# Three small experts of a mixture layer with high and low parts in one stationary operand, and a quarter of their low weights made on GpSimd

## The chip, the cores and the metric

The kernel runs on one core of a Trainium2 chip. A core has TensorE (PE) for matrix products, VectorE (DVE), ScalarE (ACT) and GpSimd (POOL) for elementwise work, and SyncE (SP), which here only issues DMAs. The metric is the device time in microseconds of one execution, as the median of several runs.

## The reference

A trunk of two layers over 256 tokens of width 1024. Each layer has a norm, an input projection, four mixers, an output projection, and then a feed-forward part: dense in layer 0, and a mixture of 8 experts in layer 1 of which each token uses two. The change is in the mixture alone:

```python
def swiglu(h, w1, w3, w2):
    return (jax.nn.silu(h @ w1) * (h @ w3)) @ w2

def moe_ffn(h, router_w, router_b, w1, w3, w2):
    logits = h @ router_w + router_b
    top_v, top_i = lax.top_k(logits, 2)
    top_w = jax.nn.softmax(top_v, axis=-1)
    combine = jnp.sum(jax.nn.one_hot(top_i, 8) * top_w[..., None], axis=-2)
    y = jnp.zeros_like(h)
    for e in range(8):
        y = y + combine[..., e:e + 1] * swiglu(h, w1[e], w3[e], w2[e])
    return y
```

Everything is float32. w1[e] and w3[e] are 1024x3584, w2[e] is 3584x1024.

## The kernel before

**Numbers of full precision.** TensorE multiplies fast in the type float32r, which keeps a part of the mantissa. So each operand is split: high is the value rounded to float32r, low is what is left. A product is then three matmuls, high·high, high·low and low·high (`three` in `one_expert`, lines L1323 to L1325).

**Tiling.** Each expert holds up to 128 tokens (`SLOTS`) as stationary operands x_high and x_low (128x128 blocks), and the weights are the moving operand, 512 columns at a time. An expert's weights are 21 chunks of 128x4096 numbers (2 MB); each chunk is two units of 128x2048, so an expert has 42 units (m = 0 to 41). Experts are taken in pairs: g is the pair (0 to 3), u the expert in it (0 or 1), and r = 2g + u. The order of a pair's units is fixed (`MOE_ORDER`): blocks of w1 and w3, with those of w2 between. `up` handles w1 and w3, `down` handles w2, `turn` transposes the gated activations so that `down` can use them as stationary operands.

**Who does what for a unit.**
- SP loads chunks into `ring`, which has 6 places; a place is free when PE has used it (`unit_used`).
- ACT makes w_high of unit m (`high`, L2547). There are 3 places for it (`HIGHS`), so ACT waits until PE has used unit m - 3.
- DVE makes the low part, ring_low = ring - w_high, 2048 columns (`low`, L2044), as soon as `high_made` says so.
- PE runs 12 matmuls of 512 columns, after `low_made`.

**Beside the units**, at numbers m written by hand in the loops of DVE and ACT (`two_experts`): ACT applies Silu to w1's sums (m = 6, 7, 15, 16, 26, 27, 36) and copies the turned activations to act_high (m = 14, 22, 34, 39); DVE multiplies with w3's sums (m = 9, 10, 18, 19, 30, 31, 37, L2105) and subtracts for act_low (m = 14, 22, 34, 39, L2110). At m = 2 and 4 DVE writes the result of the expert before, 128x1024, into act_m (L2056); GpSimd sends these rows to DRAM by an indirect DMA (`rows_out`, L842), and DVE waits at m = 9 until they have landed (`s_rows_out`), since its product at m = 9 writes act_m again. GpSimd also gathers the tokens of the next pair (`tokens_in`, L854), and in the last expert it reads the rows back, which DVE adds to x at m = 17, 20, 25, 28 (L2073). Other work GpSimd has none in this stage. The experts run in the order of their numbers.

## Time and profile before

| | |
|---|---|
| median of 3 runs | 1537.56 us (1536.78 to 1537.92) |
| profiled execution, span | 1535.7 us |
| granted TensorE clock, mean | 0.996 |
| PE busy | 1515.2 us |
| DVE busy | 1298.2 us |
| ACT busy | 968.0 us |
| POOL busy | 90.3 us |

The span is from the first to the last instruction; the timed runs lie about 1.9 us above it. The mixture's matmuls run from 559 us to the end. Ends of matmuls are modelled, so PE's busy time says little of itself; the distance from one matmul to the next shows the pace.

### The profile page before, as it was taken

How to read it: one execution, taken by the hardware profiler on the slowest of the kernel's cores; microseconds unless marked ns; L12 is line 12 of the kernel's file. 1: busy time of each engine (PE TensorE's matmuls, PEld its weight loads, DVE VectorE, ACT ScalarE, POOL GpSimd, SP SyncE). 2: the span in 40 equal slices, each digit the busy share in tenths (PEclk: the TensorE clock that was granted, in tenths of full speed). 3: DMA queues.
4: the chain of work that ended last, by engine and by line, in shares of the span. 5: the costliest groups of instructions: out<-in, count | busy, mean ns of one | idle time of the engine just before them, and what ended most of it. 6: DMA issues, size and time to landing. Idle time of an engine off the chain costs nothing.

```text
span 1535.7 us, 19169 instructions
## 1 busy us (share of the span) xinstructions
PE 1515.2 (99%) x7785; PEld 1236.0 (80%) x7785; DVE 1298.2 (85%) x1175; ACT 968.0 (63%) x841; POOL 90.3 (6%) x141
## 2 busy tenths in 40 slices
PE   8999999999999999999999999999999999999997
PEld 4886799999788568888888888888888888888885
DVE  5888887778885579988899999898998888998996
ACT  3532444444554357777777777787777787777775
POOL 5300100000000030100000100000010000000000
PEclk9999999999999999999999999999999999999999
DMA  9776698877823199999999999999999999999990
GB/s 347 285 254 239 231 359 323 304 288 274 310 94 131 55 312 391 377 385 386 354 363 385 369 392 391 354 364 382 367 390 376 376 357 375 382 364 372 411 368 30
DMA packets 161862, 494.13 MB, mean 322 GB/s; under 512 B 4587, under 2 KB 8855, under 8 KB 161767
## 3 DMA queue, kind: packets, MB, share of 16 engines
q1 hardware_dynamic: 156160, 474.76, 82.7%
q0 software_dynamic: 4928, 16.69, 3.1%
q8 instruction: 63, 1.03, 0.3%
q10 hardware_dynamic: 678, 1.40, 0.2%
q14 instruction: 33, 0.26, 0.1%
HBM read 483.91 MB, written 8.91 MB: 321 GB/s over the span
## 4 chain that ended last, share of the span: by engine, by line
PE 90%; DVE 6%; SPq 2%; DMA 1%; ACT 1%; issue 0%; DVEq 0%; ACTq 0%
PE bank L1323 20%; PE bank L1324 20%; PE bank L1325 20%; PE bank L975 4%; PE bank L1183 4%; PE bank L1224 3%; PE bank L1223 3%; PE bank L1222 3%; PE bank L972 2%; PE bank L1356 2%; PE bank L1198 1%; PE bank L1199 1%; PE bank L1200 1%; DMA ring<-in_w_mod_dram 1%; DVE ring_low L2044 1%; PE bank L998 1%
## 5 line engine op out<-in xcount | busy, mean ns | idle before, releaser
L2044 DVE TENSOR_TENSOR ring_low<-ring,w_high 128x2048 fp32r<-128x2048 f32 x336 | 768.6, 2293 | 95.1 <-ACT w_high L2547 89.0
L2547 ACT ACTIVATE w_high<-ring 128x2048 fp32r<-128x2048 f32 x336 | 646.6, 1926 | 228.8 <-PE bank L1325 220.3
L1323 PE MATMUL bank<-w_high,x_high 128*128 128x512 f32 x896 | 352.9, 394 | 0.1
L1324 PE MATMUL bank<-ring_low,x_high 128*128 128x512 f32 x896 | 351.4, 392 | 0.0
L1325 PE MATMUL bank<-w_high,x_low 128*128 128x512 f32 x896 | 348.9, 389 | 0.0
L1323 PEld LDWEIGHTS bank<-w_high,x_high 128*128 128x128 f32 x896 | 168.5, 188 | 37.4 <-DVE ring_low L2044 1.2
L1325 PEld LDWEIGHTS bank<-w_high,x_low 128*128 128x128 f32 x896 | 168.2, 188 | 37.4
L1324 PEld LDWEIGHTS bank<-ring_low,x_high 128*128 128x128 f32 x896 | 168.3, 188 | 34.7
L1323 PE MATMUL bank<-w_high,act_high 128*128 128x512 f32 x448 | 178.8, 399 | 0.2 <-DVE ring_low L2044 0.2
L2468 ACT ACTIVATE tmp_r<-ring 128x1024 fp32r<-128x1024 f32 x84 | 88.9, 1061 | 140.8 <-PE bank L1224 82.0
L1324 PE MATMUL bank<-ring_low,act_high 128*128 128x512 f32 x448 | 177.7, 397 | 0.0
L1325 PE MATMUL bank<-w_high,act_low 128*128 128x512 f32 x448 | 176.5, 394 | 0.0
L1889 DVE TENSOR_TENSOR ring_low<-ring,tmp_r 128x1024 fp32r<-128x1024 f32 x84 | 102.6, 1225 | 34.6 <-ACT tmp_r L2468 32.9
L1222 PE MATMUL bank<-h_high,tmp_r 128*128 128x256 f32 x448 | 125.7, 281 | 1.1 <-DVE h_low L1907 1.1
L1224 PE MATMUL bank<-h_low,tmp_r 128*128 128x256 f32 x448 | 125.9, 281 | 0.0
L1223 PE MATMUL bank<-h_high,ring_low 128*128 128x256 f32 x448 | 125.9, 281 | 0.0
L1323 PEld LDWEIGHTS bank<-w_high,act_high 128*128 128x128 f32 x448 | 84.2, 188 | 21.8 <-issue 0.9
L1325 PEld LDWEIGHTS bank<-w_high,act_low 128*128 128x128 f32 x448 | 84.2, 188 | 20.7
L1324 PEld LDWEIGHTS bank<-ring_low,act_high 128*128 128x128 f32 x448 | 84.2, 188 | 18.8
L1222 PEld LDWEIGHTS bank<-h_high,tmp_r 128*128 128x128 f32 x448 | 84.3, 188 | 2.4 <-issue 2.2
L1224 PEld LDWEIGHTS bank<-h_low,tmp_r 128*128 128x128 f32 x448 | 84.9, 189 | 0.0
L1223 PEld LDWEIGHTS bank<-h_high,ring_low 128*128 128x128 f32 x448 | 84.2, 188 | 0.4 <-issue 0.2
(381 smaller groups left out, 1657.3 us busy)
## 6 DMA issues: line engine op xcount, KB each, us to landing
ring<-in_moe_w_dram SPq DMA_DIRECT2D x168, 2048.0 KB, 9.1
ring<-in_w_mod_dram SPq DMA_DIRECT2D x23, 2048.0 KB, 12.9
ring<-in_ffn_w_dram SPq DMA_DIRECT2D x21, 2048.0 KB, 11.8
ring<-in_w_in_dram SPq DMA_DIRECT2D x7, 2048.0 KB, 13.6
ring<-in_w_out_dram SPq DMA_DIRECT2D x4, 2048.0 KB, 8.4
ring<-in_w_in_dram SPq DMA_DIRECT2D x4, 1024.0 KB, 15.5
ring<-in_w_mod_dram SPq DMA_DIRECT2D x2, 1024.0 KB, 15.7
gate_row<-in_b_mod_dram POOLq DMA_DIRECT2D x4, 512.0 KB, 7.6
```

What stands on the lines that cost most here:

```text
L975: ins = mm(b[:, i * T:(i + 1) * T], w[:, k, off + i * P:off + (i + 1) * P], h_t[:, k, :], start=k == 0, stop=k == KB - 1)
L1183: ins = mm(bank[2 * tt + half][:, :], y_t[:, i, tt * P:(tt + 1) * P], wide(("wout", l, half))[:, i, :], start=n == 0 and i == 2 * g, stop= ...
L1222: mm(o, w_h[:, k, :], h_high[:, k, :], start=k == 0, stop=False)
L1223: mm(o, w_l[:, k, :], h_high[:, k, :], start=False, stop=False)
L1224: ins = mm(o, w_h[:, k, :], h_low[:, k, :], start=False, stop=k == KB - 1)
L1323: mm(out_, x_h, w_h, start=first, stop=False)
L1324: mm(out_, x_h, w_l, start=False, stop=False)
L1325: return mm(out_, x_l, w_h, start=False, stop=last)
L1889: mark(tt_(quarter(ring_low, QUARTERS[m]), quarter(ring, QUARTERS[m]), quarter_high(m).bitcast(F32), ALU.subtract).then_inc(ffn_l.sem, 1), ...
L2044: tt_(moe_low(u, m // 2)[:, c], moe_slot(u, m // 2)[:, c], w_high[:, m % HIGHS, :].bitcast(F32), ALU.subtract).then_inc(low_made, 1)
L2468: mark(act(quarter_high(m), quarter(ring, QUARTERS[m]), ACT.Copy).then_inc(ffn_h.sem, 1), ffn_h, "q")
L2547: act(w_high[:, m % HIGHS, :], moe_slot(u, m // 2)[:, c], ACT.Copy).then_inc(high_made, 1)
```

## The change

- The first two experts are as before. The other six are put in an order by their number of tokens: the three with the fewest come second in the pairs 1, 2 and 3 (r = 3, 5, 7). SP reads the expert's number from memory once per expert and loads its weights from there. DVE works out the order in the first expert (`later_order`, called at m = 6 to 11).
- Such a small expert has room for 64 tokens. The stationary operand's 128 columns hold the 64 high parts and the 64 low parts of the same tokens. So two matmuls (w_high and w_low) do what three did; the result has 64 rows of high and 64 rows of low sums, which are added up later: for the gate and the product by a matmul with `fold` (128x64, two identities above each other), for the output by a second indirect DMA that adds (`compute_op=ALU.add`).
- In a small expert DVE subtracts the first 1536 columns of each unit, and GpSimd the last 512 (`low_rest`). PE waits for GpSimd's part before the last block of each unit (`rest`).
- Gate and product change: ACT copies both sums to SBUF, PE turns and adds them, ACT applies Silu to what PE made, DVE multiplies, ACT copies the high part, DVE subtracts.
- `rows_out` of a small expert is two indirect DMAs, the second issued when the first has landed; `s_rows_out` is now waited for at 16 * rows_before(r), which counts both.

```diff
+        def is_small(q, g, u):
+            return q == 0 and g > 0 and u == PAIR - 1
+        def rows_before(r):
+            return r + sum(is_small(0, n // PAIR, n % PAIR) for n in range(r))
...
+                    if later and i == 0:
+                        number_of = eng.value_load(order_i[0:1, e - FIRST:e - FIRST + 1], min_val=0, max_val=NE - 1)
...
+                if is_small(0, g, u):
+                    eng.indirect_dma_start(expert_rows[:, :], ... index[:, g % 2, 0, u, PAIR:PAIR + 1] ...)
+                    eng.wait_ge(s_rows_out, 16 * (rows_before(r) + 1))
+                    eng.indirect_dma_start(expert_rows[:, :], ... compute_op=ALU.add).then_inc(s_rows_out, 16)
...
+            def low_rest(g, u):
+                r = expert(0, g, u)
+                for m in range(UNITS):
+                    if m == ROWS_AT:
+                        rows_out(r - 1)
+                    if r == NE - 1 and m in ROWS_IN_AT:
+                        rows_in(ROWS_IN_AT.index(m))
+                    c0 = m % 2 * (KB * W // 2)
+                    c = slice(c0 + KB * W // 2 - W, c0 + KB * W // 2)
+                    eng.wait_ge(high_made, unit_at(r, m))
+                    eng.tensor_tensor(moe_low(u, m // 2)[:, c], moe_slot(u, m // 2)[:, c],
+                                      w_high[:, m % HIGHS, KB * W // 2 - W:].bitcast(F32),
+                                      ALU.subtract).then_inc(rest_made, 1)
...
+                def rest(m, last_block):
+                    if small_one and last_block:
+                        eng.wait_ge(rest_made, small_rep(g) * UNITS + m + 1)
                 def three(out_, x_h, x_l, w_h, w_l, first, last):
+                    if small_one:
+                        mm(out_, x_h, w_h, start=first, stop=False)
+                        return mm(out_, x_h, w_l, start=False, stop=last)
                     mm(out_, x_h, w_h, start=first, stop=False)
                     mm(out_, x_h, w_l, start=False, stop=False)
                     return mm(out_, x_l, w_h, start=False, stop=last)
...
                 def turn(j):
+                    if small_one:
+                        eng.wait_ge(even_a.sem, even_a.at(f"q{j}", small_rep(g)))
+                        for n, part in enumerate((act_s, act_m)):
+                            for hb in range(HB):
+                                c = n * HB * SMALL + hb * SMALL
+                                ins = mm(bank[6 + j % 2][:, c:c + SMALL], part[:, j % 2, hb * P:(hb + 1) * P], fold,
+                                         start=True, stop=True)
...
-            def low(r, u, m):
-                c = slice(m % 2 * (KB * W // 2), (m % 2 + 1) * (KB * W // 2))
+            def low(r, u, m, shared_one=False):
+                n = KB * W // 2 - (W if shared_one else 0)
+                c = slice(m % 2 * (KB * W // 2), m % 2 * (KB * W // 2) + n)
...
+                    def small_products(*js):
+                        for j in js:
+                            eng.wait_ge(moe_a.sem, moe_a.at(f"s{j}", r))
+                            done(eng, tt_(act_m[:, j % 2, 0:HB * SMALL], act_s[:, j % 2, 0:HB * SMALL],
+                                          bank[6 + j % 2][:, HB * SMALL:], ALU.mult) ...
+                        for j in js:
+                            eng.wait_ge(moe_a.sem, moe_a.at(f"ah{j}", r))
+                            done(eng, tt_(halves_of(j)[:, :, SMALL:], folded(act_m, j),
+                                          halves_of(j)[:, :, 0:SMALL].bitcast(F32), ALU.subtract) ...
...
                         if m == 9 and not first and not q:
-                            eng.wait_ge(s_rows_out, 16 * r)
+                            eng.wait_ge(s_rows_out, 16 * rows_before(r))
...
+                        if first and 6 <= m < 13:
+                            later_order(m - 6)
...
+                    def small_highs(*js):
+                        for j in js:
+                            eng.wait_ge(moe_t.sem, moe_t.at(f"t{j}", r))
+                            done(eng, act(act_s[:, j % 2, 0:HB * SMALL], bank[6 + j % 2][:, 0:HB * SMALL], ACT.Silu) ...
+                        for j in js:
+                            eng.wait_ge(moe_v.sem, moe_v.at(f"m{j}", r))
+                            done(eng, act(halves_of(j)[:, :, 0:SMALL], folded(act_m, j), ACT.Copy) ...
```

GpSimd's queue from the first gather of the mixture to the end. Before (L854 gathers tokens, L842 sends rows, L869 reads them back):

```order
L854 DMA xn<-token_rows,index 128x1024 x2
L842 DMA expert_rows<-act_m,index 640x1024 x2
L854 DMA xn<-token_rows,index 128x1024 x2
L842 DMA expert_rows<-act_m,index 640x1024 x2
L854 DMA xn<-token_rows,index 128x1024 x2
L842 DMA expert_rows<-act_m,index 640x1024 x3
L869 DMA x_slots<-expert_rows 128x2x1024 x2
```

Now, for the pairs 1 and 2 (L926 gathers, L914 sends rows, L904 and L909 are the two DMAs of a small expert, L951 is `low_rest`):

```order
L951 TENSOR_TENSOR ring_low<-ring,w_high 128x512 x6
L914 DMA expert_rows<-act_m,index 640x1024
L951 TENSOR_TENSOR ring_low<-ring,w_high 128x512 x36
L904 DMA expert_rows<-act_m,index 640x1024
L909 DMA expert_rows<-act_m,index 640x1024
L926 DMA xn<-token_rows,index 128x1024 x2
L951 TENSOR_TENSOR ring_low<-ring,w_high 128x512 x6
L914 DMA expert_rows<-act_m,index 640x1024
L951 TENSOR_TENSOR ring_low<-ring,w_high 128x512 x36
```

GpSimd, which had only DMAs to issue, has 42 subtractions per small expert, with the DMA of the expert before after six of them.

DVE's queue in the first half of a pair's second expert (u = 1). Before (L2044 is `low`, L2056 the result of the expert before, L2105 the product, L2110 act_low):

```order
L2056 TENSOR_TENSOR act_m<-bank,gate_row 128x512
L2044 TENSOR_TENSOR ring_low<-ring,w_high 128x2048 x5
L2105 TENSOR_TENSOR act_m<-act_s,bank 128x512
L2044 TENSOR_TENSOR ring_low<-ring,w_high 128x2048
L2105 TENSOR_TENSOR act_m<-act_s,bank 128x512
L2044 TENSOR_TENSOR ring_low<-ring,w_high 128x2048 x4
L2110 TENSOR_TENSOR act_low<-bank,act_high 128x512 x2
L2044 TENSOR_TENSOR ring_low<-ring,w_high 128x2048 x4
```

Now (L2215 is `low`, L2227 the result of the expert before, L2280 the product, L2285 the low part of the activations):

```order
L2227 TENSOR_TENSOR act_m<-bank,gate_row 128x512
L2215 TENSOR_TENSOR ring_low<-ring,w_high 128x1536 x10
L2280 TENSOR_TENSOR act_m<-act_s,bank 128x256 x2
L2285 TENSOR_TENSOR act_high<-act_m,act_high 128x4x64 x2
L2215 TENSOR_TENSOR ring_low<-ring,w_high 128x1536 x8
L2280 TENSOR_TENSOR act_m<-act_s,bank 128x256 x2
L2285 TENSOR_TENSOR act_high<-act_m,act_high 128x4x64 x2
```

The two products have moved from m = 9 and 10 to m = 14, just ahead of the two subtractions, and both are half as wide.

## Rows read from the trace of the kernel before

**Rows 1.** Page, part 5: engine, tiles, shapes, count; busy us, mean ns; idle before, releaser.
```profile
L2044 DVE TENSOR_TENSOR ring_low<-ring,w_high 128x2048 fp32r<-128x2048 f32 x336 | 768.6, 2293 | 95.1 <-ACT w_high L2547 89.0
L2547 ACT ACTIVATE w_high<-ring 128x2048 fp32r<-128x2048 f32 x336 | 646.6, 1926 | 228.8 <-PE bank L1325 220.3
```

**Rows 2.** Windows: stretch, us; busy of PE, PEld, DVE, ACT, POOL; clock; DMA share; GB/s.
```profile
691.10:811.50 120.40, 120.40 (x546) 98.48 (x545) 106.44 (x62) 93.14 (x67) 2.36 (x1) 1.00 0.99 368
...
700.00:710.00 10.00, 10.00 (x45) 8.23 (x44) 9.41 (x7) 6.76 (x4) 0.00 (x0) 1.00 1.03 416
```

**Rows 3.** Timeline of PE: start us, duration us, instruction; two matmuls, 32 places apart.
```profile
559.75 0.39 PE L1323 MATMUL bank<-w_high,x_high 128*128 128x512 f32 x1
...
567.07 0.39 PE L1325 MATMUL bank<-w_high,x_low 128*128 128x512 f32 x1
```

**Rows 4.** Timeline of ACT, expert r = 2: the high of m = 12.
```profile
707.35 1.93 ACT L2547 ACTIVATE w_high<-ring 128x2048 fp32r<-128x2048 f32 x1 [0.87 <-PE bank L1325]
```

**Rows 5.** Timelines of POOL, then DVE, 541 to 549 us: both subtract.
```profile
541.97 2.36 POOL L824 TENSOR_TENSOR h_high<-xn,xn_high 128x1024 fp32r<-128x1024 f32 x1 [2.12 <-PE bank L941]
544.93 3.75 POOL L824 TENSOR_TENSOR h_high<-xn,xn_high 128x1024 fp32r<-128x1024 f32 x1 [0.59 <-ACT xn_high L2361]
...
543.88 2.60 DVE L2044 TENSOR_TENSOR ring_low<-ring,w_high 128x2048 fp32r<-128x2048 f32 x1
...
547.73 0.99 DVE L1987 TENSOR_TENSOR route<-route,route_c 128x16 f32<-128x16 f32 x1
...
549.79 0.17 DVE L1987 TENSOR_TENSOR route<-route,route_c 128x16 f32<-128x16 f32 x1
```

**Rows 6.** Timelines of POOL, then DVE, 39 to 56 us: small subtractions.
```profile
39.77 0.46 POOL L797 TENSOR_TENSOR band_a<-band_a,consts 128x128 f32<-128x128 f32 x1
...
53.90 0.81 POOL L797 TENSOR_TENSOR band_b<-band_b,consts 128x128 f32<-128x128 f32 x1
...
53.69 0.69 DVE L1714 TENSOR_TENSOR tmp<-tmp 128x512 f32<-128x512 f32 x1
54.42 0.56 DVE L1718 TENSOR_TENSOR tmp<-tmp 128x256 f32<-128x256 f32 x1
55.02 0.42 DVE L1719 TENSOR_TENSOR tmp<-tmp 128x256 f32<-128x256 f32 x1
```

**Rows 7.** Timeline of DVE: an instruction with one input in PSUM beside POOL's of 541.97.
```profile
541.56 2.28 DVE L1658 TENSOR_SCALAR h_t<-bank,mod_col 128x256 f32<-128x256 f32 x4 [1.13 <-PE bank L941]
```

**Rows 8.** Timelines of ACT, then of DVE, and a group: other pieces.
```profile
558.52 0.42 ACT L2536 ACTIVATE x_high<-x_slots 128x256 fp32r<-128x256 f32 x1 [1.18 <-DVE x_slots L2184]
...
692.69 0.58 ACT L2573 ACTIVATE act_s<-bank 128x512 f32<-128x512 f32 x1
...
L2073 DVE SCALAR_TENSOR_TENSOR x<-x_slots,route_c,x 128x1024 f32<-128x1024 f32 x4 | 5.1, 1280 | 0.0
```

**Rows 9.** Timeline of DVE, expert r = 2: the product at m = 9.
```profile
703.22 0.68 DVE L2105 TENSOR_TENSOR act_m<-act_s,bank 128x512 f32<-128x512 f32 x1
```

**Rows 10.** Timeline of POOL: the row DMAs; what ended the idle time before each.
```profile
691.11 2.36 POOL L842 DMA_INDIRECT expert_rows<-act_m,index  x1 [51.87 <-DVE act_m L2056]
...
1413.17 2.34 POOL L842 DMA_INDIRECT expert_rows<-act_m,index  x1 [116.84 <-DVE act_m L2056]
1422.74 0.77 POOL L869 DMA_DIRECT2D x_slots<-expert_rows  x1 [7.24 <-DMA expert_rows<-act_m,index]
```

**Rows 11.** DMA issues: count, KB each, median us to landing; the second of these adds.
```profile
token_rows<-xn_high POOLq DMA_DIRECT2D x1, 1024.0 KB, 6.7
token_rows<-h_high POOLq DMA_DIRECT2D x1, 1024.0 KB, 8.5
```

**Rows 12.** Windows as in rows 2: 6 us during and after short pauses of PE.
```profile
552.00:558.00 6.00, 5.54 (x29) 4.71 (x29) 3.43 (x8) 2.11 (x5) 1.27 (x1) 0.72 0.54 154
```

**Rows 13.** Timeline of DVE, expert r = 0: the lows of m = 7 to 9, and of 12.
```profile
576.28 6.92 DVE L2044 TENSOR_TENSOR ring_low<-ring,w_high 128x2048 fp32r<-128x2048 f32 x3 [1.57 <-ACT w_high L2547]
...
589.21 2.29 DVE L2044 TENSOR_TENSOR ring_low<-ring,w_high 128x2048 fp32r<-128x2048 f32 x1 [0.15 <-ACT w_high L2547]
```

More of the change, by code:

```diff
@@ L206 @@
         ("lgt lg max0 eq0 cand0 first0 pick0 lg2 max1 eq1 cand1 first1 pick1 sel diff ch1 ch0 one w1 w2 sw1 sw2 wt ch2 "
-         "most most_i idle row0 row1 token0 token1").split(),
+         "count idle row0 row1 token0 token1").split(),
+    "perm_v":
+        ("key less rank lot over pos some count most most_i hot at order_f order sel2 at0 put0 at1 put1 row0 row1").split(),
+    "even_a":
+        ("p0 p1 q0 q1 p2 p3 q2 q3 p4 p5 q4 q5 p6 q6").split(),
     "route_a":
@@ L1347, in up @@
                                 for jj in range(n_j):
+                                    rest(m, (kk, jj) == (per - 1, n_j - 1))
                                     c = slice(jj * W, (jj + 1) * W)
@@ L1370, in down @@
                             for bb in range(HB // 2):
+                                rest(m, (half, bb) == (1, HB // 2 - 1))
                                 hb = part * HB // 2 + bb
@@ L1388, in last_down @@
                             for bb in range(HB // 2):
+                                rest(m, (half, bb) == (1, HB // 2 - 1))
                                 hb = part * HB // 2 + bb
@@ L2587, in two_experts @@
                                  spread_a, "s", at)
+                        if m in (10, 18, 30, 38) and small_one:
+                            j = 2 * (10, 18, 30, 38).index(m)
+                            for n in range(j, min(j + 2, NJ)):
+                                copy_value(n)
                         if m == 14:
-                            act_highs(0)
-                            act_highs(1)
+                            if small_one:
+                                small_highs(0, 1)
+                            else:
+                                act_highs(0)
+                                act_highs(1)
                         if m in (15, 16):
```

273 lines of the change are left out of this document (217 added, 56 removed).

## The prediction

> **What bounds the kernel now.** I read the page's busiest groups first, then windows of one expert each, then the timelines of PE, ACT and DVE inside a unit. An expert takes 120.35 us; six equal steps of rows like [rows 2] give that, with the clock at 1.00. Two matmuls 32 places apart start 7.32 us apart [rows 3], 0.229 us each, so a unit of 12 takes 2.745 us, and 42 units 115.3 of the 120.35; the rest is turning. ACT's high takes 1.926 us and waits for PE before nearly every unit (220 us of idle); DVE's low takes 2.293 us and waits for ACT [rows 1]. So PE sets the pace in a normal expert. DVE follows closely: 2.29 of 2.745 us. DMA moved 368 GB/s in that expert, and 416 in one stretch of 10 us [rows 2], so it isn't at its end.
>
> **What the change takes away.** In three of eight experts a unit has 8 matmuls: 8 × 0.229 = 1.83 us, 77 us an expert, with the new turns below 90. If only PE counted, each would be 30 us shorter. What is next? ACT's 1.926 us a unit, and the pair of subtractions, which is the question here.
>
> **Do DVE and GpSimd subtract side by side?** GpSimd's subtraction of 1024 columns took 2.36 us beside a DVE instruction with PSUM input, but 3.75 us when it came while DVE ran a low: that low ended at 546.48, GpSimd at 548.68, 2.20 us later. The reverse stands there too. DVE's small subtraction at 547.73 took 0.99 us instead of 0.17 and ended at 548.72, with GpSimd; and the low at 543.88, begun before GpSimd's first one ended at 544.33, took 2.60 us, ending 2.15 us after that [rows 5]. Again at 54 us: GpSimd begins at 53.90 during a DVE subtraction that ends at 54.38, and takes 0.81 us instead of 0.46; DVE's next one of 256 columns takes 0.56 instead of 0.42 and ends 0.27 us after GpSimd [rows 6]. So two subtractions with both inputs in SBUF run one after the other, whole; only the start-up (about 0.15 us each) is hidden by waiting.
>
> The Trainium skill (SBUF — State Buffer, Who interferes with whom) says that the second to issue fully blocks, but also that a DVE instruction with at most one SBUF input doesn't contend. The trace agrees: the four PSUM reads at 541.56 took 2.28 us, 0.57 each, beside GpSimd [rows 7]. By the page the new products (one input in PSUM) cost nothing beside GpSimd; counted as blocked they would add 7 × 0.42 us an expert.
>
> **Price of a unit's pair.** DVE: 2048 columns minus the start-up take 2.14 us, 1.046 ns a column, so 1536 take 1.61. GpSimd: from 128 columns in 0.46 us [rows 6] to 1024 in 2.36 [rows 5] is 2.12 ns a column, so 512 take 1.09. One after the other 2.69 us; with both start-ups unhidden 3.03; fully side by side, the longer of ACT's 1.93 and DVE's 1.76. I take 2.69, since the three blocked cases show the start-up hidden. PE has 1.83 us of work in 2.69. ACT's high of m + 3 is done 1.83 + 1.93 = 3.8 us after low m, and wanted after 6.5. So the pair sets the pace: 42 × 2.69 = 113.1 us.
>
> **The places at m = 14, 22, 34, 39.** Before, DVE multiplied at m = 9 and 10, and ACT made the next high meanwhile. Now at m = 14 DVE ends its low, multiplies (0.42), ACT copies (0.42) [rows 8, 6], twice and interleaved, about 1.4 us until ACT begins the next high; 1.93 more, then DVE's 1.7: 5.0 us from low to low instead of 2.69. That is 2.3 us, three times, and 1.8 with the single step at m = 39: 8.7 us. It could be nothing if ACT had a high in store, but it stands behind those copies in ACT's queue. Copies of the sums (14 of 0.58 us [rows 8]) fit into ACT's 0.76 us a unit and its lead; the 8 more turns per step are in PE's slack. GpSimd's DMA issue of 2.34 us at m = 6 [rows 10] lets DVE go ahead and costs about 0.7 us.
>
> Small expert: 113.1 + 8.7 + 0.7 = 122.5. r = 3 and 5 also fill the next pair's x_low, 1.1 us between lows: 123.6 each, +3.3 over 120.35. r = 7 adds the rows to x with four instructions of 1.28 us [rows 8], both inputs in SBUF, that were in slack: + 4.5, so 127.0, +6.7. Together **+13.3 us**.
>
> **The second row DMA.** Before, the rows of r = 1 were issued at 691.11 [rows 10], and DVE's wait at m = 9 ended at once, as its product began at 703.22 right behind the low [rows 9]. A row DMA lands about 9.5 us from its issue (1413.17 to 1422.74, where GpSimd waits for it) [rows 10]. After r = 3 and r = 5 the second is issued only then, and needs 9.5 us, or 11.3 if adding costs the 1.8 us by which the adding DMA to token_rows was longer [rows 11]. So DVE is free at 691.1 + 19.3 to 21.1 = 710.4 to 712.2 on the clock of r = 2. Behind its wait stand the product (0.7) and the low of m = 10 (2.29): 713.4 to 715.2. PE had finished unit 9 at 707.3, when it let ACT begin the high of m = 12 [rows 4]. PE stands still for 6.1 to 7.9 us; I take 7.7, since the new DMA adds. After short pauses of PE the granted clock was 0.72 over 6 us [rows 12]: of its two levels, 1.2 and 2.4 GHz, the lower for 3.4 us, which takes 6 × 0.28 = 1.7 us. 9.4 us, in r = 4 and r = 6: **+18.8 us**. Its bounds: nothing, if the DMAs land twice as fast; 22 with both high ends.
>
> **The order of the experts.** 21 small instructions in r = 0: 17 of 0.21 us (0.17 [rows 5] and the way to the next) and 4 on 144 numbers of 0.35, 5.0 us. After low 6 DVE idles 1.57 us [rows 13], which hides the first six; behind low 9 and before low 12 there is next to none (0.15) [rows 13], and the lead over PE is about 1 us. **+2 us** (0 to 5). SP's reads of the expert's number come many units ahead of need. The zeroing of one more block of rows and GpSimd's six new constants lie before m = 14 and are waited for by nobody earlier.
>
> **The sum.** 1535.7 + 13.3 + 18.8 + 2 = 1569.8 for the profiled span; the runs lie 1.9 above: **1571.7 us**, +2.2%.
>
> **Rivals.**
> *B, the subtractions overlap.* Then ACT bounds a small expert: 42 × 1.93 + 14 × 0.58 + 14 × 0.42 + fills of 6 = 101, with waits at the four places 104 us; 3 × -16.3 = -49, with the row DMAs' +19 and +2: **1509 us**, faster. For it: only a few overlaps are in the trace, and on GpSimd spans are rough. Against it: they all say the same, in both directions. It decides at the pair's time: with the stalls as I have them, the whole change breaks even at about 2.42 us a unit instead of 2.69, thus if a quarter of GpSimd's 1.09 us ran beside DVE.
> The Trainium skill (SBUF — State Buffer, A bandwidth-pool intuition that's wrong) gives about 358 GB/s between HBM and a core. By that an expert's 44.0 MB would take 123 us and no small expert could be shorter than before; the trace's 416 GB/s [rows 2] contradicts it, so it takes nothing from B.
> *C, nothing is hidden.* The pair takes 3.03 us: 14.3 us more per small expert, 43 in all: **1615 us**; if besides the clock fell in PE's gaps within small experts (0.9 us a unit, about 3 at the four places), a unit at half clock would be 8 × 0.43 = 3.4 us, and it is worse still. Against it: the start-ups were hidden in all cases.
> *D, a wash.* The row DMAs land early enough that DVE hardly waits, and the pair is a little faster than 2.69, down to 2.55: within 0.2%, **1537 us**.
>
> **Chances.** My forecast 0.67, B 0.15, C 0.11, D 0.07. 0.2% (3 us) is about what a measurement of this kernel can tell from no change. Faster by over 0.2%: 0.15 (B). Within: 0.07 (D). Slower: 0.78 (my forecast and C). My forecast by itself spans 1548 (no stalls beyond 3 us each, pair as taken, half the places) to 1597 (half of the start-ups unhidden). The range takes in D and most of C and leaves B out: 1534 to 1614.
>
> **What the next profile would show.** Right: in r = 3, 5, 7 GpSimd's and DVE's subtractions end alternately, low to low about 2.7 us, GpSimd's mean well over 1.3 us since it waits for DVE, or DVE's over 1.76; small experts of 122 to 127 us; r = 4 and r = 6 some 9 us longer than 120.35, with a gap on PE behind unit 9 and DVE waiting for expert_rows; r = 0 2 us longer. Wrong: DVE's lows of 1536 columns at 1.76 us and GpSimd's at 1.3 us in the same stretch, small experts near 104 us (B), or r = 4 as long as r = 2 (the second DMA is hidden).

## The result: 3.9% slower, and the profile after

| | before | after |
|---|---|---|
| median | 1537.74 us (1536.78 to 1538.52, 4 runs) | 1594.69 us (1593.5 to 1599.88, 4 runs) |
| profiled execution, span | 1535.7 us | 1597.9 us |
| granted TensorE clock, mean | 0.996 | 0.967 |
| DVE busy | 1298.2 us | 1317.5 us |
| POOL busy | 90.3 us | 390.3 us |

The ratio is 1.0385, with a 95% interval of 1.0365 to 1.0406 (the two medians by themselves give 1.037). The profiled execution of the changed kernel is the one of 1599.88 us, the slowest of its four, 5.2 us above their median. The forecast was 1571.7 us with a range of 1534 to 1614: the direction and the range hold, and the size is 23 us short.

One name in the parts ahead is wrong and touches no number. The stretch from 691 to 811 us of before, called there the expert r = 2 or its rows those of r = 1, is the expert r = 1, which sends the rows of r = 0.

I measured each expert from the second write of a result by DVE (at m = 4 of the next expert, L2056 before and L2227 after) to the next such write. For r = 7 the interval ends in the same way at the last result. In us:

| r | 1 | 2 | 3 small | 4 | 5 small | 6 | 7 small |
|---|---|---|---|---|---|---|---|
| before | 121.2 | 119.6 | 121.2 | 119.7 | 121.2 | 119.2 | 111.1 |
| after | 121.0 | 118.9 | 134.0 | 128.5 | 133.8 | 129.4 | 126.5 |

The differences add up to the 62.2 us between the two profiled spans: 1.9 before the mixture's first matmuls, 2.2 in r = 0, 12.8 + 12.6 + 15.4 = 40.8 in the small experts, 8.8 + 10.2 = 19.0 in r = 4 and r = 6, and -1.7 in the rest.

The groups of the page of after that answer to [rows 1] (columns as there; "+1 forms" means that two shapes share the row). L2215 is DVE's `low`, L951 GpSimd's `low_rest`, L1424 PE's first matmul in a small expert:

```profile
L2215 DVE TENSOR_TENSOR ring_low<-ring,w_high 128x2048 fp32r<-128x2048 f32 (+1 forms) x336 | 785.2, 2353 | 113.8 <-ACT w_high L2751 108.4
L2751 ACT ACTIVATE w_high<-ring 128x2048 fp32r<-128x2048 f32 x336 | 641.7, 1920 | 237.0 <-PE bank L1428 164.4
L951 POOL TENSOR_TENSOR ring_low<-ring,w_high 128x512 fp32r<-128x512 f32 x126 | 293.9, 2350 | 266.6 <-ACT w_high L2751 265.4
...
L1424 PE MATMUL bank<-w_high,x_high 128*128 128x512 f32 x336 | 146.4, 436 | 55.0 <-DVE ring_low L2215 49.7
```

The same groups by shape, from 560 to 1600 us, after:

```profile
L2215 DVE TENSOR_TENSOR ring_low<-ring,w_high 128x2048 fp32r<-128x2048 f32 x207 | 473.5, 2292 | 56.1 <-ACT w_high L2751 52.1
L2215 DVE TENSOR_TENSOR ring_low<-ring,w_high 128x1536 fp32r<-128x1536 f32 x126 | 304.8, 2454 | 55.6 <-ACT w_high L2751 54.2 <-DMA expert_rows<-act_m,index 0.5
```

DVE has a quarter fewer columns in a small expert and yet takes longer for them: 2454 ns for 1536, against 2292 for 2048. That is time in which the instruction stands and waits for GpSimd, as in the few cases of [rows 5]. The timelines of DVE, then of POOL, in r = 3 show it (start us, duration us, instruction, count; in brackets the idle time ahead of it and what ended it):

```profile
950.59 10.83 DVE L2215 TENSOR_TENSOR ring_low<-ring,w_high 128x1536 fp32r<-128x1536 f32 x4 [0.25 <-ACT w_high L2751]
961.35 0.86 DVE L2280 TENSOR_TENSOR act_m<-act_s,bank 128x256 f32<-128x256 f32 x2
962.37 0.95 DVE L2285 TENSOR_TENSOR act_high<-act_m,act_high 128x256 fp32r<-128x256 f32 x2 [0.16 <-ACT act_high L2798]
964.77 8.37 DVE L2215 TENSOR_TENSOR ring_low<-ring,w_high 128x1536 fp32r<-128x1536 f32 x3 [1.45 <-ACT w_high L2751]
973.41 1.76 DVE L2215 TENSOR_TENSOR ring_low<-ring,w_high 128x1536 fp32r<-128x1536 f32 x1 [0.28 <-ACT w_high L2751]
```

```profile
964.75 1.27 POOL L951 TENSOR_TENSOR ring_low<-ring,w_high 128x512 fp32r<-128x512 f32 x1 [2.17 <-ACT w_high L2751]
...
973.46 2.87 POOL L951 TENSOR_TENSOR ring_low<-ring,w_high 128x512 fp32r<-128x512 f32 x1 [1.93 <-ACT w_high L2751]
```

Not held up, DVE's instruction takes 1.76 us (973.41) and GpSimd's 1.27 (964.75). GpSimd's of 973.46 begins 0.05 us after DVE's, and ends 1.16 us after it, having taken 2.87. In the steady stretch at 950.59 four lows take 10.83 us: 2.70 us a unit, where 1.76 + 1.27 is 3.03, so 0.33 us of start-up is hidden.

### The profile page after: what moved, and what is told of

Its sections match the earlier page's. It is cut to its first block, busy times and chain, and to the rows that moved or that the text cites. A ratio compares the mean times of both kernels' runs of the same rounds, so it can differ in the third digit from the quotient of the medians.

```text
span 1597.9 us, 19147 instructions
## 1 busy us (share of the span) xinstructions
PE 1479.0 (93%) x7533; PEld 1189.2 (74%) x7533; DVE 1317.5 (82%) x1199; ACT 978.0 (61%) x883; POOL 390.3 (24%) x276
## 4 chain that ended last, share of the span: by engine, by line
PE 65%; DVE 14%; ACT 7%; DMA 5%; POOL 4%; issue 4%; SPq 1%; ACTq 0%; DVEq 0%; POOLq 0%
PE bank L1426 10%; PE bank L1427 10%; PE bank L1428 10%; DVE ring_low L2215 10%; PE bank L1068 5%; ACT w_high L2751 4%; DMA expert_rows<-act_m,index 4%; PE bank L1276 4%; POOL ring_low L951 3%; PE bank L1317 3%; PE bank L1316 3%; PE bank L1315 3%; PE bank L1065 3%; PE bank L1424 2%; PE bank L1425 1%
## 5 line engine op out<-in xcount | busy, mean ns | idle before, releaser
L2215 DVE TENSOR_TENSOR ring_low<-ring,w_high 128x2048 fp32r<-128x2048 f32 (+1 forms) x336 | 785.2, 2353 | 113.8 <-ACT w_high L2751 108.4
L951 POOL TENSOR_TENSOR ring_low<-ring,w_high 128x512 fp32r<-128x512 f32 x126 | 293.9, 2350 | 266.6 <-ACT w_high L2751 265.4
L1426 PE MATMUL bank<-w_high,x_high 128*128 128x512 f32 x560 | 223.1, 398 | 17.3 <-DVE ring_low L2215 17.0
L1427 PE MATMUL bank<-ring_low,x_high 128*128 128x512 f32 x560 | 221.4, 395 | 0.0
L1428 PE MATMUL bank<-w_high,x_low 128*128 128x512 f32 x560 | 219.7, 392 | 0.0
L1424 PE MATMUL bank<-w_high,x_high 128*128 128x512 f32 x336 | 146.4, 436 | 55.0 <-DVE ring_low L2215 49.7
L1425 PE MATMUL bank<-ring_low,x_high 128*128 128x512 f32 x336 | 139.7, 416 | 0.0
L1426 PEld LDWEIGHTS bank<-w_high,x_high 128*128 128x128 f32 x560 | 106.4, 190 | 43.0 <-DVE ring_low L2215 19.3
L1424 PEld LDWEIGHTS bank<-w_high,x_high 128*128 128x128 f32 x336 | 68.2, 203 | 87.4 <-DVE ring_low L2215 63.8
L1428 PEld LDWEIGHTS bank<-w_high,x_low 128*128 128x128 f32 x560 | 106.1, 190 | 23.9
L1427 PEld LDWEIGHTS bank<-ring_low,x_high 128*128 128x128 f32 x560 | 106.3, 190 | 21.8
L1428 PE MATMUL bank<-w_high,act_low 128*128 128x512 f32 x280 | 110.8, 396 | 0.0
L1426 PE MATMUL bank<-w_high,act_high 128*128 128x512 f32 x280 | 110.6, 395 | 0.0
L1427 PE MATMUL bank<-ring_low,act_high 128*128 128x512 f32 x280 | 109.5, 391 | 0.0
L1424 PE MATMUL bank<-w_high,act_high 128*128 128x512 f32 x168 | 77.1, 459 | 25.7 <-DVE ring_low L2215 25.6
```

The source lines that it names most:

```text
L951: eng.tensor_tensor(moe_low(u, m // 2)[:, c], moe_slot(u, m // 2)[:, c], w_high[:, m % HIGHS, KB * W // 2 - W:].bitcast(F32), ALU.subtract ...
L1424: mm(out_, x_h, w_h, start=first, stop=False)
L1425: return mm(out_, x_h, w_l, start=False, stop=last)
L1426: mm(out_, x_h, w_h, start=first, stop=False)
L1427: mm(out_, x_h, w_l, start=False, stop=False)
L1428: return mm(out_, x_l, w_h, start=False, stop=last)
```

## What takes the 13 us of a small expert: a sum along DVE

From the result of r = 2 to that of r = 3 (933.5 to 1067.6 us), DVE's timeline of after divides so:

| stretch | by the measured pair of 2.70 us | measured |
|---|---|---|
| 10 lows, m = 5 to 14 | 27.0 | 27.1 |
| 8 lows, m = 15 to 22 | 21.6 | 21.7 |
| 12 lows, m = 23 to 34, with two subtractions for x_low | 32.4 | 37.2 |
| 5 lows, m = 35 to 39, with the third | 13.5 | 15.8 |
| 3 lows, m = 40 and 41 and the next expert's m = 0 | 8.1 | 8.1 |
| places behind m = 14, 22, 34, 39 | | 3 x 3.42 + 2.99 = 13.3 |
| the next expert's first 4 lows and results | | 10.9 |

The total is 134.1. The pair's pace is as forecast. Two lines are not: the places cost 13.3 us where 8.7 stood in the sum, and the stretches m = 23 to 39 lose 7.1 us where 1.1 stood for the fills. (The forecast's 0.7 us for GpSimd's DMA issue belongs to the first stretch, and nearly none of it shows there.)

**A place.** The rows above show it: DVE's low of m = 14 ends at 961.3, then two products, two subtractions, and 1.45 us of waiting for ACT's next high; the next low begins at 964.77. That is 3.42 us in which no low runs. The low of m = 15 then takes 2.86 us, since GpSimd's of 964.75 began just ahead of it.

**The long stretch.** ACT makes the next pair's tokens there ("fills"). Its timeline of after, r = 3, and DVE's beside it:

```profile
1014.58 1.15 ACT L2728 ACTIVATE x_slots<-bank,mod_col 128x256 f32<-128x256 f32 x2
1015.76 1.91 ACT L2751 ACTIVATE w_high<-ring 128x2048 fp32r<-128x2048 f32 x1
1017.58 1.15 ACT L2728 ACTIVATE x_slots<-bank,mod_col 128x256 f32<-128x256 f32 x2
1018.76 1.91 ACT L2751 ACTIVATE w_high<-ring 128x2048 fp32r<-128x2048 f32 x1
```

```profile
1014.71 1.76 DVE L2215 TENSOR_TENSOR ring_low<-ring,w_high 128x1536 fp32r<-128x1536 f32 x1 [1.23 <-ACT w_high L2751]
1017.71 1.76 DVE L2215 TENSOR_TENSOR ring_low<-ring,w_high 128x1536 fp32r<-128x1536 f32 x1 [1.24 <-ACT w_high L2751]
1020.70 1.76 DVE L2215 TENSOR_TENSOR ring_low<-ring,w_high 128x1536 fp32r<-128x1536 f32 x1 [1.24 <-ACT w_high L2751]
1022.38 2.98 DVE L2180 TENSOR_TENSOR x_low<-x_slots,x_high 128x256 fp32r<-128x256 f32 x2
```

ACT is at work without a pause: a high and two fills are 3.0 us, and so the lows come every 3.0 us. DVE waits 1.24 us for each high; its low then takes 1.76 us, unblocked. Then the two subtractions for x_low, both inputs in SBUF, take 2.98 us instead of the 0.88 that they take where GpSimd subtracts nothing (the first experiment below): GpSimd's subtraction stands in their way too.

A part of the loss is neither. Ahead of these rows, at m = 26 to 28, the lows come 3.6 to 3.7 us apart, and there ACT's highs waited for PE, which was behind after a stretch at the lower clock (0.50 from 992 to 998 us):

```profile
996.66 1.91 ACT L2751 ACTIVATE w_high<-ring 128x2048 fp32r<-128x2048 f32 x1 [3.30 <-PE bank L1425]
...
1000.35 1.93 ACT L2751 ACTIVATE w_high<-ring 128x2048 fp32r<-128x2048 f32 x1 [1.29 <-PE bank L1425]
```

What the clock takes in these stretches is measured by the matmuls at the places, below.

## Experiments: which part costs what

Two things had to be told apart: whether the shared run of the two subtractions sets the pace or the wait of PE for GpSimd, and what fills the rest of the 13 us. Each quoted expectation gives its own theories.

**GpSimd subtracts nothing.** VectorE takes all 2048 columns; the rest of the change stays.

```diff
+SHARE = 0
...
-                    eng.tensor_tensor(moe_low(u, m // 2)[:, c], moe_slot(u, m // 2)[:, c], ...
...
-                    if small_one and last_block:
-                        eng.wait_ge(rest_made, small_rep(g) * UNITS + m + 1)
...
-                n = KB * W // 2 - (W if shared_one else 0)
+                n = KB * W // 2 - (SHARE if shared_one else 0)
```

> In the three small experts VectorE subtracts all 2048 columns of a unit and GpSimd none; PE waits for VectorE alone. Nothing else is changed. Theory 1 (the two subtractions take turns at one SBUF port, 1.61 + 1.09 = 2.7 us a unit): VectorE alone needs 2.25 us a unit, so 42 x 0.45 = 19 us less in each small expert, 3 us more where GpSimd no longer holds up the fills; about 1530 us, faster than the changed kernel by 60. Theory 2 (the subtractions run side by side, and the copies at m = 14, 22, 34, 39 with their clock falls are what costs): VectorE has a third more to do in each unit and GpSimd's part was free, so it is slower than the changed kernel or the same, 1595 us or more.

It took 1544.83 us (1543.76 to 1546.0), ratio to before 1.0051 (1.0034 to 1.0068): 50 us less than the change, and 15 above the 1530 that its first theory gave. The small experts took 117.3, 117.8 and 106.8 us. So the subtraction on GpSimd is what makes them slow, although GpSimd takes work off DVE. They are also only 3 to 4 us shorter than before the change, although PE has a third less to do. DVE's lows in r = 3:

```profile
L2209 DVE TENSOR_TENSOR ring_low<-ring,w_high 128x2048 fp32r<-128x2048 f32 x43 | 96.7, 2288 | 13.5 <-ACT w_high L2745 13.0
```

DVE's own 96.7 us are now the larger part of the expert, and of the 13.5 us of idle time nearly all is for ACT's highs.

**GpSimd subtracts 256 columns instead of 512.**

```diff
+SHARE = 256
...
-                    c = slice(c0 + KB * W // 2 - W, c0 + KB * W // 2)
+                    c = slice(c0 + KB * W // 2 - SHARE, c0 + KB * W // 2)
...
-                n = KB * W // 2 - (W if shared_one else 0)
+                n = KB * W // 2 - (SHARE if shared_one else 0)
```

> GpSimd subtracts 256 columns of each unit in the small experts instead of 512, VectorE 1792 instead of 1536. Theory 1: the pair takes 1.87 + 0.54 = 2.41 us instead of 2.70, so 12 us less in each small expert, about 1560 us, between the changed kernel and the one where VectorE subtracts all. Theory 2: no gain, 1595 us or a little more.

1569.38 us (1564.45 to 1572.9), ratio 1.0207 (1.0179 to 1.0236), small experts 122.9, 124.0 and 114.3 us: 10 to 12 us less each, near the 12 expected, and the run 9 us above the 1560. Half the share costs about half of the 50 us. POOL's group, from 560 to 1600 us, shows that most of the instruction is waiting: half the columns take 1887 ns instead of 2350.

```profile
L952 POOL TENSOR_TENSOR ring_low<-ring,w_high 128x256 fp32r<-128x256 f32 x126 | 236.3, 1887 | 292.5 <-ACT w_high L2752 291.8
```

**GpSimd subtracts beside, and nobody waits for it.** VectorE takes all 2048 columns. GpSimd subtracts 512 columns of two other tiles once a unit; its result isn't used. Its first one in each small expert waits until PE has ended the expert before.

```diff
-                    eng.tensor_tensor(moe_low(u, m // 2)[:, c], moe_slot(u, m // 2)[:, c], ...
+                    eng.tensor_tensor(y_low[:, 0:W], gate_row[:, 0:W], final_row[:, 0:W],
                                       ALU.subtract).then_inc(rest_made, 1)
```

> The changed kernel with VectorE subtracting all 2048 columns of a unit, while GpSimd, once a unit in r = 3, 5, 7, subtracts 512 columns of two other tiles in SBUF (gate_row and final_row) into a tile that is not in use; nobody on PE's side waits for it and its result isn't used. It measures what GpSimd's subtraction costs VectorE when neither data nor a wait of PE ties the two. Theory 1 (the two engines' instructions with both inputs in SBUF run one after the other): a unit takes 2.14 + 1.09 = 3.23 us, small experts about 136 to 142, VectorE's lows show up to 3.4 us, and the run takes 1544.8 + 55 to 65 = 1600 to 1610. Theory 2 (they read side by side, and the change loses by PE's wait for a slow GpSimd): lows stay at 2.29 and the run at 1545, as with GpSimd subtracting nothing.

**The same with a memset**, which reads nothing.

```diff
-                    eng.tensor_tensor(y_low[:, 0:W], gate_row[:, 0:W], final_row[:, 0:W], ALU.subtract)
+                    eng.memset(y_low[:, 0:W].bitcast(F32), 0.0)
```

> As the run beside it, but GpSimd's instruction is a memset of 512 columns: it reads nothing from SBUF, only writes. The result isn't used. Theory 1 in its narrow form (only instructions with two SBUF inputs block each other): 1545, as with GpSimd doing nothing in these units. If any GpSimd instruction blocks VectorE, or its waits and semaphores cost by themselves, the small experts lengthen as in the run beside it, by its own duration of some 0.5 us a unit: 1565 and above.

Beside the subtraction the run takes 1652.51 us (1645.63 to 1653.86), ratio 1.0735 (1.0701 to 1.077), with small experts r = 3 and 5 of 149.8 and 147.7 us. Beside the memset it takes 1546.39 us (1544.69 to 1548.06), ratio 1.006 (1.0041 to 1.008), as with GpSimd doing nothing. From 960 to 1560 us, first POOL and DVE beside the subtraction, then beside the memset:

```profile
L954 POOL TENSOR_TENSOR act_low<-gate_row,final_row 128x512 fp32r<-128x512 f32 x96 | 253.9, 2645 | 210.4 <-ACT w_high L2754 202.2
...
L2216 DVE TENSOR_TENSOR ring_low<-ring,w_high 128x2048 fp32r<-128x2048 f32 x179 | 488.7, 2762 | 37.4 <-ACT w_high L2754 35.4
```

```profile
L954 POOL MEMSET act_low<- 128x512 f32 x110 | 57.9, 527 | 373.1 <-ACT w_high L2753 372.6
...
L2215 DVE TENSOR_TENSOR ring_low<-ring,w_high 128x2048 fp32r<-128x2048 f32 x194 | 438.7, 2289 | 58.7 <-ACT w_high L2753 56.3
```

With no common data and no wait of PE, GpSimd's subtraction of two SBUF tiles still lengthens DVE's lows; writing alone leaves them at 2289 ns. In a steady stretch eight lows beside the subtraction took 26.5 us, 3.31 a unit, near the sum of the two (2.14 + 1.09 = 3.23). The kernel lost more than the 55 to 65 us expected, 108 over the run in which GpSimd did nothing, and again not by the pair's pace: 38 lows at 3.31 are 125.8 us, and with the 13.3 us of the places and the next expert's start of 10.9 they give the 150 us that r = 3 took. The expectation had left the last two nearly out.

**Copies one unit later.** ACT copies the high activations, and DVE subtracts for the low ones, behind the next high and low (m = 15, 23, 35, 40), so that the next high doesn't stand behind them.

```diff
+                        if small_one and m in (15, 23, 35, 40):
+                            j = 2 * (15, 23, 35, 40).index(m)
+                            small_copies(*range(j, min(j + 2, NJ)))
```

> In the small experts ScalarE copies the high part of the gated activations, and VectorE subtracts for the low part, one unit later: behind the high and the low of m = 15, 23, 35 and 40. Silu and product stay where they are. Theory A (ScalarE's next high stood behind a copy that waits for VectorE's product, so VectorE and PE ran dry and the clock fell): the gaps of about 2.3 us at four places and the half clock behind them go, 12 to 16 us less in each small expert, 1548 to 1558 us; the granted clock stays near 1.0 in them. Theory B (the pace of the subtractions is all there is): under 5 us in all, 1590 to 1595 us.

1579.07 us (1576.13 to 1580.96), ratio 1.0274 (1.0253 to 1.0294): 16 us less than the change, between the two expectations. Small experts 126.2, 127.2 and 121.6 us. A place with it, DVE, r = 3:

```profile
959.05 0.86 DVE L2280 TENSOR_TENSOR act_m<-act_s,bank 128x256 f32<-128x256 f32 x2
960.53 2.88 DVE L2215 TENSOR_TENSOR ring_low<-ring,w_high 128x1536 fp32r<-128x1536 f32 x1 [0.62 <-ACT w_high L2756]
963.34 0.87 DVE L2287 TENSOR_TENSOR act_high<-act_m,act_high 128x256 fp32r<-128x256 f32 x2
```

Two products and the wait are 1.48 us instead of 3.42, and the subtractions come back as 0.9 to 2 us behind the low. The lows of the long stretch still come every 3.0 us. The small experts lose 7.8, 6.6 and 4.9 us of the 12.8, 12.6 and 15.4 by which they had grown: 61, 52 and 32%. Not all of that is the place's order by itself: without the stops at the places the granted clock in r = 3 is 0.99 instead of 0.91, and what that is worth comes below.

**A tile of its own for the rows.** The small expert's result goes to DRAM from another tile (it lies in the place of act_low, which is free until m = 14 of the next expert), and DVE's wait for the row DMAs moves to m = 14.

```diff
                 rows = act_m[:, :, :].rearrange("p a n -> p (a n)")
                 if is_small(0, g, u):
+                    rows = row_tile[:, :, :].rearrange("p a n -> p (a n)")
...
-                        if m == 9 and not first and not q:
+                        if m == (14 if is_small(0, (r - 1) // PAIR, (r - 1) % PAIR) else 9) and not first and not q:
```

> The rows of the experts r = 3 and 5 go out from the place of act_low, which is free until m = 14 of the next expert, and VectorE waits for the two row DMAs at m = 14 instead of m = 9 there. Theory: the wait is over by then, PE's gap behind unit 9 of r = 4 and r = 6 and the half clock behind it go, 9 to 10 us each, about 1576 us. If the two DMAs cost in another way (through the DMA engines, or GpSimd's queue), there is no gain, 1595 us.

1575.79 us (1573.28 to 1579.84), ratio 1.0249 (1.0232 to 1.0267), 19 us less, as expected. r = 4 and r = 6 are 118.9 and 118.5 us instead of 128.5 and 129.4; the small experts stay at 134.0, 133.7 and 126.5. DVE at m = 9 and 10 of r = 4, of after and then of this run:

```profile
1079.05 2.32 DVE L2215 TENSOR_TENSOR ring_low<-ring,w_high 128x2048 fp32r<-128x2048 f32 x1 [0.37 <-ACT w_high L2751]
1089.00 0.69 DVE L2294 TENSOR_TENSOR act_m<-act_s,bank 128x512 f32<-128x512 f32 x1 [7.63 <-DMA expert_rows<-act_m,index]
```

```profile
1079.35 2.29 DVE L2219 TENSOR_TENSOR ring_low<-ring,w_high 128x2048 fp32r<-128x2048 f32 x1 [0.37 <-ACT w_high L2756]
1081.56 0.68 DVE L2299 TENSOR_TENSOR act_m<-act_s,bank 128x512 f32<-128x512 f32 x1
```

**The clock, by two more matmuls a unit.** Behind each place PE's matmuls start 0.43 us apart, the pace at 1.2 GHz, for some units: in r = 3 that is about 24 us in all (a mean of 0.91 over 134 us, between the levels 0.50 and 1.00). Three matmuls of after behind the first place, and a window behind the second (columns as in [rows 2]):

```profile
967.68 0.79 PE L1424 MATMUL bank<-w_high,x_high 128*128 128x512 f32 x1 [3.38 <-DVE ring_low L2215]
968.27 0.63 PE L1425 MATMUL bank<-ring_low,x_high 128*128 128x512 f32 x1
968.70 0.63 PE L1424 MATMUL bank<-w_high,x_high 128*128 128x512 f32 x1
```

```profile
992.00:994.00 2.00, 1.22 (x3) 1.04 (x4) 2.00 (x2) 1.36 (x1) 2.00 (x2) 0.50 1.03 396
```

PE had stood still for 3.4 us ahead of the first. Does the lower clock cost anything? Zeros as a stationary operand keep PE busier without changing a sum. GpSimd writes the zeros at the start of each small expert, when PE has ended the expert before; n counts the blocks of matmuls, four in a unit.

```diff
+                    if m == 0:
+                        eng.wait_ge(unit_used, used_at(r, -1))
+                        eng.memset(act_low[:, 0, 0:P].bitcast(F32), 0.0).then_inc(s_clear, 1)
...
                     if small_one:
                         mm(out_, x_h, w_h, start=first, stop=False)
...
+                        if n % 4 in (1, 2):
+                            mm(out_, act_low[:, 0, 0:P], w_h, start=False, stop=False)
```

> The changed kernel with two more matmuls in each unit of r = 3, 5, 7: a stationary operand of zeros, made by GpSimd once an expert in act_low (which a small expert doesn't use), against w_high, added into the same sums, so nothing that is computed changes. PE's work in a unit goes from 1.83 to 2.29 us at the full clock, still below the 2.70 us of the pair of subtractions. Theory C (the clock at 1.2 GHz behind PE's stops costs time by itself: in r = 3 it lasts about 24 us in all, in which a unit takes 3.44 us instead of 2.70, so 7 units lose 0.74 each): with its stops shorter PE keeps the clock of 2.4 GHz and each small expert is about 5 us shorter, 129 instead of 134, the run about 1579 to 1584. Theory L (the clock only falls where PE would wait anyway, and what costs is that ACT and VectorE have no lead): no gain, or 0 to 5 us more per small expert since PE catches up less: 1595 to 1610.

> The same two matmuls with zeros per unit, on the kernel whose copies and subtractions of the activations come one unit later (1579.1 without them; r = 3, 5, 7 of 126.2, 127.2, 121.6 us, and the lower clock over about 4 us only in r = 3). There is next to no half clock left to win, so by both theories 1577 to 1584; if filling PE's gaps brings as much here as on the changed kernel itself, then it isn't by the clock.

On the changed kernel 1602.8 us (1601.24 to 1603.95), ratio 1.0441 (1.0423 to 1.0458), with small experts of 132.7, 133.9 and 127.2; on the one with later copies 1595.42 us (1592.72 to 1596.2), ratio 1.0392 (1.0375 to 1.0409), with 130.6, 128.9 and 126.8 instead of 126.2, 127.2 and 121.6. The first is where theory L had it. The second missed its expectation by 11 us and spoils the first as a proof: the edit costs something itself where there is next to no low clock to win back. So the extra matmuls were put only where PE stands still.

**The clock, by matmuls at the places only.** 12 matmuls with zeros before units 15, 23 and 35, 8 before unit 40; GpSimd writes the zeros as before.

```diff
+                            if small_one and m in (15, 23, 35):
+                                keep_busy(bank[first][:, :], 12)
                             eng.wait_ge(low_made, unit_at(r, m))
...
+                    if small_one and 2 * i == 40:
+                        keep_busy(bank[4][:, :], 8)
```

> The changed kernel; in r = 3, 5, 7 PE gets matmuls with zeros only where it stands still at the four places (12 of 0.229 us before unit 15, 23 and 35, 8 before unit 40, moving operand x_high, added into the sums, so nothing that is computed changes). Two matmuls in every unit kept the clock but cost PE's catching up elsewhere; these lie in stops of about 3.4 us. If the clock behind the places costs what the stretches behind m = 22 and m = 34 showed with the clock kept (1.7 and 0.8 us shorter), each small expert is 2 to 3 us shorter and the run 1586 to 1589 where the changed kernel again takes 1594.7. If half clock is hidden (the pair of subtractions is the pace at either clock), it takes the same within 2 us.

> The changed kernel as it is, on the same chip beside the run with matmuls at the places: 1594.7 as before (1593.5 to 1599.9), small experts of 134.0, 133.8, 126.5 us.

1595.89 us (1589.26 to 1600.35) with them, 1594.24 (1591.62 to 1596.53) without, ratios to before 1.0385 (1.0355 to 1.0415) and 1.0371 (1.0351 to 1.0391). One window over r = 3 of each, with them and then without (columns as in [rows 2]):

```profile
934.40:1064.80 130.40, 111.45 (x520) 85.84 (x521) 116.83 (x63) 97.05 (x81) 85.04 (x39) 1.00 0.92 341
```

```profile
932.10:1066.20 134.10, 109.16 (x476) 84.85 (x477) 109.64 (x63) 96.90 (x81) 91.07 (x39) 0.91 0.89 334
```

The clock stays at 1.00 instead of 0.91, and this expert is 3.7 us shorter. All of it lies in the two stretches m = 23 to 34 and 35 to 39: 34.6 and 14.5 us instead of 37.1 and 15.8. In r = 5 (0.97 instead of 0.91) the same two stretches are 3.3 us shorter together, and the expert takes 132.4 instead of 134.2. In r = 7, where ACT makes no fills, they take 49.7 and 49.4 us, so nothing is won, though the clock is 0.95 instead of 0.90, and the expert takes 127.7 instead of 125.3.

The edit has a price of its own that hides the gain in the sum. The interval of r = 2 ends four units into r = 3, where GpSimd waits and writes the zeros: it is 120.1 us instead of 118.9, and 120.2 in both runs with two more matmuls a unit. In r = 5 and r = 7 the stretch m = 5 to 14 is 1.1 us longer than without, and DVE waits there for the row DMA, which it doesn't without (1.80 and 1.65 us). Over the whole run nothing is won that can be measured: the expected 1586 to 1589 was missed, and the two runs are within 2 us, as if the half clock were hidden, though in two experts it isn't. So in r = 3 and r = 5 the lower clock takes part in the loss, with 3.3 to 3.7 of the 13 us, each from one profiled execution; it isn't the main cause. Of the 7.1 us lost in r = 3 at m = 23 to 39, 3.2 are left with the clock kept.

**Three edits together.** GpSimd subtracts nothing, copies one unit later, a tile of its own for the rows: the diffs above.

> Three edits of the changed kernel at once: VectorE subtracts all 2048 columns of a unit and GpSimd none; ACT's copies of the high activations and VectorE's subtraction for the low ones come one unit later (m = 15, 23, 35, 40); the row before goes through a tile of its own, and VectorE waits for the rows at m = 14 instead of m = 9. Everything is computed. By the single edits: GpSimd subtracting nothing gave 1544.8 with experts r = 3, 5, 7 at 117.3, 117.8, 106.8 us; a tile of its own took 9.5 and 10.9 us from r = 4 and r = 6; the later copies took 7.8, 6.6 and 4.9 us from the small experts, of which part hung on the shared port. If the effects add: 1544.8 - 20 = 1525 with the tile, and 3 to 15 us less with the copies, so 1510 to 1522, which is below the kernel of before (1537). If VectorE (2.14 to 2.29 us a unit, 90 to 96 us an expert, and its products) is the bound of a small expert by itself, the copies bring nothing and it is 1525. Rival: the gaps return elsewhere and it stays at 1537 or above.

1522.35 us (1520.42 to 1523.04), ratio 0.99 (0.9877 to 0.9924): faster than before by 1%, just above the 1510 to 1522 expected, and 72 us faster than the change. The experts are 121.0, 119.0, 115.5, 119.0, 115.8, 118.6 and 105.8 us. The gains add: the row tile's 20 us, and 2 us more by the copies, which bring little once the shared subtraction is gone. The window over r = 3:

```profile
933.50:1049.10 115.60, 101.74 (x477) 77.50 (x477) 102.22 (x62) 96.82 (x81) 2.36 (x1) 1.00 1.01 387
```

PE, DVE and ACT are each busy for 97 to 102 of 115.6 us, and the DMA engines' share is 1.01. No engine waited for a DMA in this window, and SP, which issues the loads, waited 105.6 us in it for PE to free places of the ring. DVE waited 12.8 us for ACT's highs, and ACT 13.8 for PE. No engine's work alone explains the rest of the time; which of them would have to be relieved next wasn't tried.

## Why the prediction was right in kind and too small

- **That PE sets the pace before, by little: borne out.** With GpSimd's part gone, a third less work for PE shortened a small expert by 3 to 4 us only, and DVE's lows and ACT's highs wait for each other. The new places are in that number too.
- **That two subtractions with both inputs in SBUF run one after the other: right**, in both directions, and it doesn't need common data or a wait. The rule of the Trainium skill (SBUF — State Buffer, Who interferes with whom), that the second to issue is fully blocked, holds here with 1.27 us becoming 2.87. So does its other half: DVE's two products at 961.35, with one input in PSUM, took 0.86 us while GpSimd's subtraction, held back by the low before them, ran on until 962.6.
- **2.69 us a unit: right.** 2.70 was measured in steady stretches, so 0.33 us of start-up is hidden, as taken. Rival B (side by side, 1509) and rival C's own mechanism (no start-up hidden, 3.03 us) are both out.
- **The four places, 8.7 us: too small.** They took 13.3 us. The step that failed is "1.93 more, then DVE's 1.7: 5.0 us from low to low instead of 2.69". The time without a low was nearly right, 1.4 + 1.93 = 3.3 us where 3.42 was measured. But the low behind the place was priced as if it had no partner. GpSimd waited for the same high and began first (964.75), and DVE's low took 2.86 us, not 1.7. So a place costs its whole 3.42 us on top of the pace, and not 2.3.
- **Fills, 1.1 us: too small.** 7.1 us were lost in the stretches with fills. Two things stand behind it. The step "1.1 us between lows" counted DVE's fills at their unblocked price and left out ACT's, which with the high take 3.0 us a unit there; DVE's three x_low subtractions took 4.75 us in r = 3. That is 3.2 us, the loss that was left with the clock kept. The rest, 3.7 to 3.9 us, went with the lower clock behind the places, which the sum put at nothing.
- **r = 7, +6.7 us: too small**, at +15.4. The places count here too, 4.6 us more than forecast. Its four additions to x, with both inputs in SBUF, had been priced at 1.28 us each, and two of them were held up by GpSimd's subtractions, 2.1 us in all (mean 1801 ns instead of 1280). The last 2 us weren't broken down.

```profile
L2246 DVE SCALAR_TENSOR_TENSOR x<-x_slots,route_c,x 128x1024 f32<-128x1024 f32 x4 | 7.2, 1801 | 0.0
```

- **The second row DMA, 9.4 us each in r = 4 and r = 6: right**, 8.8 and 10.2, and 9.6 and 10.9 by the run with the tile of its own. DVE was expected free at 19.3 to 21.1 us after the first DMA's issue. In r = 4 POOL issued it at 1069.14, and DVE went on at 1089.00, 19.9 us later, 9.9 for each of the two. In r = 6 it was 22.1 us, above that range: 10.0 for the first and 12.0 for the adding one, whose issue on GpSimd took 3.63 us instead of 1.56. In the repeated run both pairs took 19.9 and 19.8. So adding costs nothing in some cases and about 2 us in others; what decides it stays open.

```profile
1069.14 2.33 POOL L904 DMA_INDIRECT expert_rows<-act_m,index  x1 [15.84 <-DVE act_m L2227]
1079.05 1.56 POOL L909 DMA_INDIRECT expert_rows<-act_m,index  x1 [7.59 <-DMA expert_rows<-act_m,index]
```

PE stood still for 6.78 us before its next matmul (7.7 had been taken), and the rest of the 8.8 is what came behind: the granted clock was 0.50 from 1092 to 1096 us and 0.65 in the 2 us after (1.7 us had been taken for it, and 2.0 are left of the 8.8).

```profile
1092.07 0.80 PE L1426 MATMUL bank<-w_high,x_high 128*128 128x512 f32 x1 [6.78 <-DVE ring_low L2215]
```

- **The order of the experts, +2 us: right.** From the mixture's first matmul to the result of r = 0 it is 132.7 us instead of 130.6. The 1.9 us ahead of the mixture differ from run to run: 0.4 in the repeated run of the changed kernel, and with GpSimd subtracting nothing the mixture's first matmuls came 1.8 us earlier than before the change.
- **The lower clock inside small experts** stood only in a clause of rival C. It does occur, in r = 3 for some 24 us, and costs 3.7 us there and 3.3 in r = 5, in stretches where ACT has no lead; in r = 7 nothing was won by keeping it up. The mean clock of 0.967 shows PE's waiting more than it explains the loss.

The small experts took 40.8 us more instead of 13.3, which is 27.5 of the 28.1 us between the forecast span of 1569.8 and the profiled one of 1597.9. The profiled execution lay 5.2 us above the median, and so the medians' miss is 23. The direction was right for the reason given. That the time lay in the range is partly luck: its upper end came from rival C and the forecast's own span up to 1597 from half of the start-ups unhidden, and neither happened; the places, the fills and the clock filled that room.

## What to carry to other kernels

Here, work moved from VectorE to GpSimd saved nothing, since the instructions of both read two SBUF operands: the pair took the sum of the two, less the start-up, and VectorE's other such instructions in the same stretch got longer too. Before giving GpSimd a share, ask which of VectorE's instructions read an input from PSUM, as the products here, which were not held up, and let those lie beside it. And when an engine stops being the bound, go through every other engine's smaller pieces again at the new pace: what stood in the slack of 2.745 us a unit (ACT's fills, copies ahead of the next high, a second DMA behind the first) has to be priced in full.

## What the runs showed of the hardware that was not expected

- GpSimd's write of 512 columns (0.53 us) costs VectorE nothing beside it (lows of 2289 ns), while its subtraction of the same width does (2762 ns). The prediction hadn't asked; the narrow form of that experiment's theory had it so. A GpSimd instruction with a single SBUF input wasn't run.
- The indirect DMA that adds took 9.95 us from its issue to DVE going on in r = 4 and 12.0 in r = 6 of the same execution, where the plain ones ahead of them took 9.9 and 10.0.
- Extra matmuls in PE's waiting time weren't free: 0.46 us of them a unit, with the zeros that GpSimd writes for them, cost 16 us with the later copies, 11 of them in the small experts, though PE's 2.29 us stayed below the 2.70 us of the pair. How much of it is the matmuls and how much GpSimd's wait at each expert's start wasn't settled.
- A higher granted clock isn't by itself a gain: 1.00 instead of 0.91 gave 3.7 us in r = 3, and 0.95 instead of 0.90 nothing in r = 7.
